# Three edits around a fast-multiplication MLP in a fused decoder trunk: a later finish for two jobs, first products kept in PSUM, first three products by K quarters

## The reference, cut to what matters

```
hn = rms_norm(h, mlp_norm[i])
h = h + jnp.square(jax.nn.relu(hn @ w_mlp_in[i])) @ w_mlp_out[i]
```

## Time and profile before

| | us |
|---|---|
| median of 3 runs | 2432.41 (2431.59 to 2433.84) |
| the profiled execution, its own time | 2426.45 |
| its span, first to last instruction | 2424.7 |
| PE busy / DVE / POOL / ACT | 2288.2 / 1681.8 / 1087.3 / 923.7 |
| first MLP's matmuls | 540.2 to 1173.7 |
| second MLP's matmuls | 1641.3 to 2280.2 |
| mean granted PE clock | 0.977 |

### The profile page before, as it was taken

How to read it: one execution, slowest core, us unless ns; L and a number is a source line. 1 busy time by engine, 2 the same in 40 slices (tenths; PEclk the granted TensorE clock), 3 DMA queues, 4 the chain that set the end, 5 groups by cost and what they waited for, 6 DMA issues and landing times.

```text
span 2424.7 us, 31481 instructions
## 1 busy us (share of the span) xinstructions
PE 2288.2 (94%) x12286; PEld 1845.0 (76%) x12286; DVE 1681.8 (69%) x1967; ACT 923.7 (38%) x1438; POOL 1087.3 (45%) x684
## 2 busy tenths in 40 slices
PE   8998976999999989999998999998999989999997
PEld 6887855787788868888786776676788868888786
DVE  6869178569787887569717355568877796678815
ACT  4120146435333344334313145655333343344315
POOL 4433122135555555556332244564555545566421
PEclk9998988999999999999999999999999999999998
DMA  7382342212443644533113111021435375335111
GB/s 212 99 124 70 108 136 74 88 52 72 154 156 135 225 178 157 191 121 123 53 44 110 38 27 61 19 87 35 157 135 186 142 249 174 123 138 174 44 43 70
DMA packets 226086, 277.87 MB, mean 115 GB/s; under 512 B 33573, under 2 KB 172041, under 8 KB 221833
## 3 DMA queue, kind: packets, MB, share of 16 engines
q1 hardware_dynamic: 212392, 257.14, 32.1%
q10 hardware_dynamic: 13552, 18.81, 3.1%
HBM read 190.53 MB, written 84.21 MB: 113 GB/s over the span
## 4 chain that ended last, share of the span: by engine, by line
PE 76%; DVE 16%; issue 3%; ACT 2%; DMA 1%; ACTq 1%; POOL 0%; DVEq 0%; SPq 0%; POOLq 0%
PE ps L1205 42%; PE ps L828 15%; PE ps L1371 3%; PE ps L979 2%; PE ps L1403 2%; PE ps L1331 1%; DVE hg_queries_keys L2288 1%; PE ps L1344 1%; PE ps L1355 1%; DVE stage L1950 1%; PE ps L1000 1%; PE ps L1015 1%; DVE st_lo L2453 1%; PE ps L895 1%; DVE quads L2473 1%
## 5 line engine op out<-in xcount | busy, mean ns | idle before, releaser
L1205 PE MATMUL ps<-op,st_hi 128*128 128x512 f32 x3584 | 1113.7, 392 | 34.3 <-DVE st_lo L2453 24.1
L1205 PEld LDWEIGHTS ps<-op,st_hi 128*128 128x128 f32 x3584 | 674.9, 189 | 185.1 <-DVE st_lo L2453 29.5
L1205 PE MATMUL ps<-op,st_lo 128*128 128x512 f32 x1792 | 700.5, 391 | 0.0
L672 POOL TENSOR_TENSOR st_lo<-st_raw,st_hi 128x512 fp32r<-128x512 f32 x192 | 312.1, 1626 | 497.1 <-ACT st_hi L1454 495.2
L1205 PEld LDWEIGHTS ps<-op,st_lo 128*128 128x128 f32 x1792 | 338.2, 189 | 71.2
L633 POOL CAST w_hi<-w_raw 128x1024 fp32r<-128x1024 f32 x66 | 73.5, 1114 | 485.9 <-issue 250.0
L1454 ACT ACTIVATE st_hi<-st_sum 128x512 fp32r<-128x512 f32 x256 | 159.9, 628 | 311.4 <-POOL st_sum L664 124.3
L1454 ACT ACTIVATE st_hi<-st_raw 128x512 fp32r<-128x512 f32 x192 | 120.9, 630 | 360.2 <-PE ps L1205 175.8
L2453 DVE TENSOR_TENSOR st_lo<-st_sum,st_hi 128x512 fp32r<-128x512 f32 x256 | 236.8, 931 | 7.4 <-ACT st_hi L1454 6.1
L2517 DVE TENSOR_TENSOR residual<-residual,ps 128x512 f32<-128x512 f32 x192 | 130.4, 681 | 122.6 <-PE ps L1205 122.1
L2533 DVE TENSOR_TENSOR op<-op_raw,op 128x1024 fp32r<-128x1024 f32 x112 | 176.2, 1574 | 16.6 <-ACT op L1454 16.6
(11 more groups left out here) (341 smaller groups left out, 3473.6 us busy)
## 6 DMA issues: line engine op xcount, KB each, us to landing
op_raw<-mid_dram SPq DMA_DIRECT2D x56, 1024.0 KB, 7.5
st_raw<-w_mlp_in_in SPq DMA_DIRECT2D x32, 1024.0 KB, 5.6
mid_dram<-quads SPq DMA_DIRECT2D x32, 1024.0 KB, 3.9
st_raw<-w_mlp_out_in SPq DMA_DIRECT2D x32, 1024.0 KB, 5.4
mid_dram<-mid_sums SPq DMA_DIRECT2D x32, 512.0 KB, 3.5
w_raw<-w_in_even_in SPq DMA_DIRECT2D x20, 512.0 KB, 4.6
residual_dram<-residual ACTq DMA_DIRECT2D x2, 4096.0 KB, 12.4
mid_dram<-mid_last_sum SPq DMA_DIRECT2D x32, 256.0 KB, 2.4
```

What stands on the lines that cost most here:

```text
L672: pool.tensor_tensor(SL[r][:, :, :], x, SH[r][:, :, :].bitcast(F32), sub).then_inc(S["st_lo_pool"], 1)
L1205: ins = pe.matmul(PS[:, o, :], w[:, j, :], OP[s][:, x, j, :], start=(fresh and j == 0 and w is SH[r] and x == 0), stop=(j == 3 and w is SL ...
```

## The change

It does three things in both MLPs.

1. The steps that finish jobs 14 and 15 (`scaled`, `squared`, mid sums, stores) come nine slots later (`TURN`), t = 120 to 127 in place of 111 to 118. For all other jobs `post` gives the same slots as before.
2. For q = 0 and 1 product 0 of the four rounds adds up in bank d (`resident`). Product 3 starts fresh in bank a. Nothing is taken out until the last round, where `evict_down` adds bank d to all four blocks of H. The copies of jobs 20 and 21 and the additions of product 0 of the other rounds go.
3. At the start PE runs K quarters 0 to 2 of products 0, 1 and 2, then quarter 3 of the three. Around that the orders of ACT and DVE are rewritten: the last two `add_squares` go behind the operands, `sum_squares` goes behind product 4, `late_difference` reads H itself (four DVE instructions, so ACT's `x_late` for s = 4 goes; the sign is turned in `third_sum`), and it and the first half of `late_last` come ahead of the read of the sum of squares, while the second half comes behind `block_low(4)`, four evictions and two `weight_low`.

```diff
+TURN = 9
+def resident(g, s):
+    return s == 0 and g >= UP and (g - UP) % 4 < 2
+def post(t):
+    last = UP * SLOTS - 1
+    return divmod(t + 1 if t < last else t + 1 - TURN if t >= last + TURN else 0, 2 * SLOTS)
-COPIES = counted([(2 * k + b, 0) for k in (*range(SETS // 2), SETS // 2 + 1, SETS // 2 + 2) for b in range(2)])
+COPIES = counted([(2 * k + b, 0) for k in (*range(SETS // 2), SETS // 2 + 1) for b in range(2)])
...
@@ SP: stores @@
-                    if 1 <= k <= SETS // 2:
-                        if r == 3:
-                            store_set(g - 2)
...
+                    kp, rp = post(t)
+                    if 1 <= kp <= SETS // 2:
+                        first, second = 2 * kp - 2, 2 * kp - 1
+                        if rp == 4:
+                            store_set(first)
...
@@ POOL: third_sum @@
+                    ends = (quarter(g, 1, 0), quarter(g, 0, 0)) if g < UP else (quarter(g, 0, 0), quarter(g, 1, 0))
@@ PE: bank @@
-                    elif s == 0:
+                    elif resident(g, s):
+                        if g < UP + 2:
+                            pe.wait_ge(S["st_ev"], ev(i, g - 2, 3))
+                    elif s == 0 or s == 3 and resident(g, 0):
...
@@ PE: products @@
+                    o = (d_ if resident(g, s) else a_, b_, c_, d_ if g < UP else a_, b_, c_, b_)[s]
+                    fresh = g < UP + 2 if resident(g, s) else s < 3 or s == 3 and (g < UP or resident(g, 0))
...
+                for steps in ((0, 1, 2), (3,)):
+                    for n in range(3):
+                        product(n, steps)
+                for n in range(3, PRODUCTS):
+                    product(n, range(4))
+                    if n == 4:
                         sum_squares(norm)
@@ ACT: start @@
-                x_operands(i, norm, 7)
                 high(3)
                 high(4)
+                x_operands(i, norm, 7)
+                x_late(i, 5)
+                x_square(norm, 7)
                 high(5)
                 high(6)
-                x_late(i, 4, 0)
+                x_late(i, 6)
                 high(7)
-                x_late(i, 5, 1)
-                x_late(i, 6, 1)
+                copy(0, 0)
                 cast_late(i, 4, 9, 9)
-                copy(0, 0)
                 copy(1, 0)
...
-                        if r == 0:
-                            squared(g - 2)
-                        if r == 2:
-                            squared(g - 1)
+                    kp, rp = post(t)
+                    if 1 <= kp <= SETS // 2 and rp in (1, 3):
+                        squared(2 * kp - 2 + rp // 2)
@@ DVE: operands, evictions @@
-                    add_squares(norm, m)
...
-                    tt(OPF[4][:, 1, :, :], OPF[5][:, 1, :, :], OPF[4][:, 1, :, :], sub).then_inc(S["op_x_sum"], 1)
+                    for j in range(4):
+                        ins = dve.scalar_tensor_tensor(OPF[4][:, 1, j, :], H[:, 2 * j, rights], col("mlp", KT * i + 2 * j), OPF[5][:, 1, j, :],
+                                                       ALU.mult, sub)
...
+                    z = PS[:, d_, :] if resident(g, 0) else Z1[q][:, :]
...
-                    if s == 0 and c == 0:
-                        tt(h12, h12, PS[:, a_, :], add)
-                        tt(h22, h22, PS[:, a_, :], add)
-                        tt(h21, h21, PS[:, a_, :], add).then_inc(S["st_ev"], 1)
-                        return
...
+                    if c == 3 and s == 4 and resident(g, 0):
+                        dve.wait_ge(S["st_ev"], ev(i, g, 3))
+                        own(tt(h11, h11, z, add))
@@ DVE: start @@
+                    if m == KT - 1:
                         weight_low(2)
                     x_residual(m)
                     x_lows(m - 1)
+                    if m < KT - 1:
+                        add_squares(norm, m - 1)
                     x_sum(m)
+                weight_low(3)
                 x_lows(KT - 1)
+                weight_low(4)
+                add_squares(norm, KT - 2)
+                add_squares(norm, KT - 1)
                 end_norm()
-                weight_low(4)
                 weight_low(5)
+                late_difference()
+                late_first()
                 dve.wait_ge(S["ss_done"], norm + 1)
                 dve.tensor_scalar(RSTD[:, :], ...)
-                late_difference()
+                for s in (1, 2):
+                    evict_up(0, s)
+                block_low(4, 17)
+                weight_low(8)
+                for s in (1, 2):
+                    evict_up(1, s)
+                weight_low(9)
                 late_last()
-                block_low(4, 17)
-                for g in range(2):
-                    for s in (1, 2):
-                        evict_up(g, s)
-                    weight_low(8 + g)
                 block_low(5, 18)
@@ DVE: finish @@
-                    if k < SETS // 2 and r == 13:
-                        scaled(g)
...
+                    kp, rp = post(t)
+                    if 1 <= kp <= SETS // 2:
+                        first, second = 2 * kp - 2, 2 * kp - 1
+                        if rp == 0:
+                            scaled(first)
+                        if rp == 1:
+                            scaled(second)
+                        if rp == 3:
+                            first_mid_sums(first)
...
```

More of the change, by code:

```diff
@@ L93 @@
 SUMS = counted([e for k in range(SETS) for e in both(k, (2, 1, 4, 5), ((2, 1), (4,), (5,)))])
-COPIES = counted([(2 * k + b, 0) for k in (*range(SETS // 2), SETS // 2 + 1, SETS // 2 + 2) for b in range(2)])
+def resident(g, s):
[4 more added lines that the diff above has]
+COPIES = counted([(2 * k + b, 0) for k in (*range(SETS // 2), SETS // 2 + 1) for b in range(2)])
 EVICTIONS = counted([e for k in range(SETS // 2) for e in both(k, (), ((1, 2), (3,), (4,), (5,), (6,)))]
-                    + [product_at(n) for n in range(UP * SLOTS, PRODUCTS) if product_at(n) not in COPIES])
+                    + [product_at(n) for n in range(UP * SLOTS, PRODUCTS) if product_at(n) not in COPIES and not resident(*product_at(n))])
 ROW = dict(mix=0, mlp=16, ple=32, final=48, head_norm=56, b_glu=60, lb=64, lam_re=68, lam_im=84)
@@ L260, in build @@
     T4 = at("mid_last_sum", [P, HALF], F32, E0_AT + 12 * K)
-    Z1 = [at(f"p1_sum{q}", [P, HALF], F32, E1_AT + (8 + 2 * q) * K) for q in range(4)]
+    Z1 = {q: at(f"p1_sum{q}", [P, HALF], F32, E1_AT + (4 + 2 * q) * K) for q in (2, 3)}
     def dram(name, shape):
@@ L1193, in operand, with product @@
                         pe.wait_ge(S["op_ready"], n + X_READY + 14 * ((g - UP) // 4) + 2 * s + j // 2 + 1)
-                for n in range(PRODUCTS):
+                def product(n, steps):
                     g, s = product_at(n)
                     a_, b_, c_, d_ = BANKS[g % 2]
-                    o, r = (a_, b_, c_, d_ if g < UP else a_, b_, c_, b_)[s], n % RINGS
-                    fresh = s < 3 or s == 3 and g < UP
-                    weights(g, s)
-                    bank(g, s)
-                    for j in range(4):
+                    r = n % RINGS
+                    o = (d_ if resident(g, s) else a_, b_, c_, d_ if g < UP else a_, b_, c_, b_)[s]
+                    fresh = g < UP + 2 if resident(g, s) else s < 3 or s == 3 and (g < UP or resident(g, 0))
+                    if 0 in steps:
+                        weights(g, s)
+                        bank(g, s)
+                    for j in steps:
                         operand(g, s, j)
@@ L1711, in x_operands @@
                     first, second = 1, 3
-                act.wait_ge(S["sq_used"], m + 8 * norm + CREDIT)
-                fn(SQ[:, :], H[:, m, :], ACT.Square).then_inc(S["sq_done"], 1)
+                if m < KT - 1:
+                    x_square(norm, m)
                 act.wait_ge(S["op_x_scaled"], X_SCALED * i + m + 1)
@@ L1810, in mlp @@
                 cast_late(i, 6, 10, 11)
-                high(10)
-                high(11)
-                high(12)
-                high(13)
+                for n in range(10, 14):
+                    high(n)
                 for t in range(10, PRODUCTS + 1):
@@ L2511, in evict_down @@
                         return
-                    if (g, 0) not in COPIES and c == 0:
-                        dve.wait_ge(S["st_ev"], ev(i, g, 0))
                     if s in (4, 5):
@@ L2551, in mlp @@
                 for m in range(1, KT):
-                    if i and m == KT - 1:
+                    if m == KT - 1:
                         weight_low(2)
@@ L2600, in mlp @@
                         evict_up(g - 1, 6)
-                    if t > UP * SLOTS and product_at(t - 1) not in COPIES:
+                    if t > UP * SLOTS and product_at(t - 1) in EVICTIONS:
                         evict_down(*product_at(t - 1))
```

71 lines of the change are left out of this document (33 added, 38 removed).

## The result

The changed kernel takes 2418.3 us (median of 4, 2416.03 to 2419.06) against 2432.28 for the kernel before (4 runs beside them): ratio 0.994 [0.9923, 0.9957]. The forecast was 2406.3, and its range ended at 2414.5: of the 26.1 us forecast, 12 did not come. The sign was right.

What follows compares the result with a forecast made beforehand. PE was taken to wait mostly for DVE's low parts of weights, at the turn and start. 13.1 + 12.5 + 1.1 + 1.6 - 2.2 = 26.1 us off 2426.45 gives 2400.4, plus 6.0 for the median 2406.3; range 2398 to 2414.5.

Steps and rivals of the forecast that it cites:

- The turn, 13.1 and 12.5: Turn to the down projection, up to product 120: PE's lost time returns, 13.1 us in the first MLP, 12.5 in the second.
- One sign: Expected in the trace at the turn: DVE with idle time in 860 to 877 after the shift.
- The moved work ... I take nothing: Slots t = 120 to 127: 14.0 us of moved DVE work fits into 21.8 us beside some 8; charged nothing.
- The start, +1.1 and +1.6: Start of each MLP, up to `scaled(0)`: square root done earlier, a gain of 1.1 us and 1.6 us.
- The path behind `late_last`: Start: raw load, six POOL instructions, `high(17)`, table load and square root follow `late_last`; 21.5 us with hand-overs.
- the end of `late_last`: DVE at the start: `late_last` ends some 2.1 and 1.3 us later than before, at 566.0 and 1672.5.
- my upper bound: DVE at the start: `late_difference` in four pieces of 0.67 us takes at most 2.7 us.
- The gap before product 22, "near 4 us": Start of each MLP: PE waits again about 4 us before product 22, uncertain by 1 us.
- The clock, -2.2: Behind the gap before product 22: half speed charged once of two times, 2.2 us lost.
- the turn held by the next in line: Rival: casts, loads or POOL's third sum hold product 120, leaving 7.1 us lost per MLP; 2420.5 us, chance 0.1.
- clock and load path against the start: Rival: half speed after both gaps (4.4 us) and POOL's six instructions slow (4.8 in all); 2413.3 us, chance 0.2.
- the slower case: Rival: moved work stalls PE before product 128, 16.2 us per MLP; 8.5 us slower, 2440.9 us, chance 0.02.

Runs made afterwards that it cites:

- Twelve slots: Parts 1 and 2 of the change without part 3, jobs 14 and 15 finished twelve slots later, not nine (TURN = 12): 2407.64 us, 0.9902 of the kernel before.
- the square root first: Changed kernel with the square root put ahead of `high(17)` in ACT's order: 2410.35 us, 0.9913 of the kernel before.

## Why the prediction was wrong

- **The turn, 13.1 and 12.5: right.** Measured 13.4 and 12.2. PE waited at most 0.63 us from product 113 to 121, at full clock. One sign failed in the first MLP: DVE had no idle time in 860 to 877, though 17.9 us had been taken away for 10.9. It only just kept up. In the second it had 2.9 us, all of them waits for ACT.
- **"The moved work ... I take nothing": failed, 6.7 us.** The step set 14.0 us of moved work plus "some 8" against the 21.8 us of slots 120 to 127, as if DVE began them level with PE. That is 22 us of work for 21.8, with nothing to spare; and DVE was 6.8 and 7.0 us behind, since the turn up to product 120 had become 11 us shorter while the refills, nine of 1.81 us (16.3) in 862 to 885, still had to fit. The text named 2 to 6 us per MLP if the mid sums were slow, and the sum and the range took none. Twelve slots took back about half of the loss (1.7 of 3.3); what the other half is made of is open but for 0.7 us of waiting for POOL. The comparison with the earlier trace rows misled: there DVE had its idle time because PE had been late before, 4.94 us at product 120.
- **The start, +1.1 and +1.6: failed, 7 us.** The path behind `late_last` was right to 0.2 us in the first MLP and 0.3 in the second. The term that failed is the end of `late_last`, put 3.5 and 3.3 us too early. Three things make it up. I let what precedes it start 4.9 us earlier, which took the read of the sum of squares (1.2) out of DVE's queue, though the change only moves it within the queue. The four pieces took 4.8 for the 2.7 of my upper bound. And `late_difference` began 1.0 and 1.2 later than put: in the first MLP DVE sat idle 1.20 us for the last `Square` behind `x_late(5)`, which I had charged in the second alone; in the second its last low part took 1.56 us, where three had taken 1.90. Evictions and low parts between overlap by 0.6 in all, so 3.7 for 3.5 in the first, and 3.9 for 3.3 in the second. The run with the four pieces in one, and that with the square root first, show that `late_last` and the square root do set product 22.
- **The gap before product 22, "near 4 us": 2.5 and 2.1.** PE reached it later, as product 6 waited first. That wait was not in the working; its removal alone changed the time by nothing.
- **The clock, -2.2: 1.5 us in the second MLP, but for the wrong reason.** The gap lengths that I sorted by don't decide below 3.2 us: with the square root first, 2.45 and 2.44 before product 22 were followed by half speed in both MLPs, while 2.45 in the changed kernel was not, and 2.6 before product 8 went either way in the same code. In all profiled executions every gap of 4.78 us or more was followed by half speed. I can't say what decides between.
- **The rivals.** The one nearest in time (the turn held by the next in line, 2420.5) did not happen: no gap stands before product 120, so its nearness is luck. The next (clock and load path against the start, 2413.3) charged 4.8 for POOL's six instructions, and these came as forecast. None held a loss behind the turn short of the slower case, whose mechanism, work that stalls PE where it lands, is the one that happened, at 3.3 us per MLP in place of 16.2.

Together, by the stages of the first table: 26.1 - 6.7 (behind the turn) - 7.1 (start) + 0.9 (22 to 112: -1.35 in place of -2.2) + 0.5 (132 to the end) = 13.7, the two MLPs' 8.2 and 5.5.

## What to carry over

When a wait of PE is taken away, the engine that was behind it doesn't get faster: the work between has to fit into a shorter time, and a deadline that was met before has to be checked with the backlog carried forward, slot by slot. When an order is rewritten, write out the new queue of the engine from a fixed start with every instruction in it; the shift of one instruction against its old place loses those that were only moved. And look at the far side of a long full stretch as well: a gain of 2.4 us at product 22 was lost 90 products later, where one sum a slot later, with its store, had pushed back two loads that were due there.

## What the runs showed of the hardware

DVE's price of an operation depends on its inputs and on POOL. Within the changed kernel's turn, first the view of the evictions (min, median and max in ns), then two mid sums in DVE's timeline:

```profile
L2540 DVE TENSOR_TENSOR residual<-residual,ps x12: 671/674/682, 872.4 to 906.8; 128x512 f32<-128x512 f32 x12
```

```profile
899.65 1.78 DVE L2513 TENSOR_TENSOR quads<-quads 128x512 f32<-128x512 f32 x1
...
903.06 0.68 DVE L2513 TENSOR_TENSOR quads<-quads 128x512 f32<-128x512 f32 x1
```

All twelve operations with one input in PSUM take 0.67 to 0.68, ten of them while POOL ran all the time; the same size with both inputs in SBUF takes 0.68 with POOL idle (903.06) and up to 1.78 beside it (899.65). The pieces of `late_difference` were 0.74, 0.74, 1.76 and 1.77. The Trainium skill ("SBUF — State Buffer", Who interferes with whom) says just this: two SBUF inputs contend with a GpSimd instruction that reads SBUF, one does not. The trace agrees. What it adds here is up to 1.1 us for an instruction, whatever its size: 0.68 to 1.78 for 512 columns, 1.21 to 2.31 for the refills' 1024. So work with two SBUF inputs that is moved beside POOL should be priced with up to 1.1 us more for each instruction. POOL pays too: its instructions in the turn take 1.29 to 2.29.

Executions of these kernels also differ by 3 us ahead of the first MLP, in code that is the same: product 0 starts at 540.2 in some profiled executions and at 542.9 to 543.9 in others, of both forms of the start. Between the MLPs the same happens again (467.6 us before, 470.9 after). Together what lies outside the MLPs took 1151.4 us in the shortest of the profiled executions and 1159.1 in the longest. That is more than most of the differences between experiments here. So stages were compared and not spans, and a median of four to six runs, which holds this too, is no finer scale for a step of 2 or 3 us.
